# Splitting the projection weights in pieces of 512 columns, and taking the top-k passes ahead of two conv slabs

## What is computed

```python
(u_pool, c_a, c_g, d_q, d_k, d_v, i_q, i_k, i_w,
 n_q, n_ck, n_cv, n_sk, n_sv, n_wk, n_wv, n_g) = jnp.split(x @ w_in[l], IN_OFFSETS, axis=-1)
y_pool = _pool_mixer(u_pool, ...)            # trailing means over 2/4/8/16 tokens
y_conv = _conv_module(c_a, c_g, ...)         # a*sigmoid(g), causal depthwise conv of width 31, LN, silu, pointwise
y_dsa = _dsa_attention(d_q, d_k, d_v, i_q, i_k, i_w, slopes_dsa)  # top 128 keys by a ReLU indexer
y_nsa = _nsa_attention(...)
mix = jnp.concatenate([y_pool, y_conv, y_dsa, y_nsa], axis=-1)
x = _layernorm(DN_ALPHA * x + mix @ w_out[l], ln1_g[l], ln1_b[l])
gate, up = jnp.split(x @ w_gate_up[l], 2, axis=-1)
x = _layernorm(DN_ALPHA * x + (jax.nn.silu(gate) * up) @ w_down[l], ln2_g[l], ln2_b[l])
```

## Time and profile before

| | |
|---|---|
| times of three runs | 2241.58, 2241.82, 2243.14 us |
| median | 2241.82 us |
| span of the profiled execution | 2238.2 us |
| PE busy | 2139.7 us (96%) |
| DVE busy | 650.7 us (29%) |
| POOL busy | 1258.1 us (56%) |
| ACT busy | 195.1 us (9%) |

### The profile page before, as it was taken

The page is one execution under the profiler, slowest core; times in us unless marked ns, Lnnn a source line. Parts: engine busy times, 40 slices in busy tenths (PEclk is TensorE's granted clock), DMA queues, the critical chain, the costliest instruction groups (busy, mean ns, idle before and its releaser), DMA issues.

```text
span 2238.2 us, 23796 instructions
## 1 busy us (share of the span) xinstructions
PE 2139.7 (96%) x9593; PEld 1742.9 (78%) x9593; DVE 650.7 (29%) x1017; ACT 195.1 (9%) x380; POOL 1258.1 (56%) x447
## 2 busy tenths in 40 slices
PE   8999996399999899999999999999999999999996
PEld 7778885266788788888888888888888888888885
DVE  1037999747100811102011120201111020110217
ACT  2020000046000300000000000000000000000001
POOL 6536665016366366555556656565555656666565
PEclk9999998699999999999999999999999999999998
DMA  6323334021423232333333233332333333232332
GB/s 186 96 74 95 94 94 113 0 81 39 169 94 100 89 94 94 94 96 94 105 98 95 94 94 94 94 94 94 95 103 94 101 94 94 94 94 94 94 94 94
DMA packets 290049, 212.64 MB, mean 95 GB/s; under 512 B 7478, under 2 KB 254070, under 8 KB 288218
## 3 DMA queue, kind: packets, MB, share of 16 engines
q1 hardware_dynamic: 289930, 211.97, 31.8%
q10 hardware_dynamic: 80, 0.13, 0.0%
HBM read 207.76 MB, written 4.19 MB: 95 GB/s over the span
## 4 chain that ended last, share of the span: by engine, by line
PE 84%; DVE 14%; issue 1%; ACT 0%; POOL 0%; DMA 0%; DVEq 0%; POOLq 0%; ACTq 0%
PE psum L580 17%; PE psum L582 16%; PE psum L581 16%; DVE proj L1260 7%; PE psum L917 7%; PE psum L918 7%; PE psum L916 7%; PE psum L811 2%; PE psum L813 2%; PE psum L812 2%; DVE sel L1243 1%; DVE top L1242 1%; PE psum L791 1%; PE psum L729 1%; DVE acc L1472 1%; PE psum L703 1%
## 5 line engine op out<-in xcount | busy, mean ns | idle before, releaser
L457 POOL TENSOR_TENSOR w_lo<-raw,w_hi 128x2048 fp32r<-128x2048 f32 (+1 forms) x175 | 822.0, 4697 | 14.6
L454 POOL TENSOR_SCALAR w_hi<-raw 128x2048 fp32r<-128x2048 f32 (+1 forms) x175 | 338.7, 1935 | 792.7 <-PE psum L582 512.4
L580 PE MATMUL psum<-act_hi,w_hi 128*128 128x512 f32 (+1 forms) x1984 | 764.3, 385 | 5.3 <-DVE act_lo L1192 2.2
L582 PE MATMUL psum<-act_hi,w_lo 128*128 128x512 f32 (+1 forms) x1984 | 762.3, 384 | 0.0
L581 PE MATMUL psum<-act_lo,w_hi 128*128 128x512 f32 (+1 forms) x1984 | 762.2, 384 | 0.0
L580 PEld LDWEIGHTS psum<-act_hi,w_hi 128*128 128x128 f32 x1984 | 372.8, 188 | 82.0 <-DVE act_lo L1480 2.7
L581 PEld LDWEIGHTS psum<-act_lo,w_hi 128*128 128x128 f32 x1984 | 372.7, 188 | 74.9 <-issue 0.5
L582 PEld LDWEIGHTS psum<-act_hi,w_lo 128*128 128x128 f32 x1984 | 372.5, 188 | 74.4
L1517 DVE TENSOR_TENSOR hid<-psum,silu_g 128x512 f32<-128x512 f32 x44 | 30.5, 692 | 840.9 <-PE psum L582 840.9
L918 PE MATMUL psum<-w_lo,h_hi 128*128 128x512 f32 x640 | 253.1, 396 | 0.0
L917 PE MATMUL psum<-w_hi,h_lo 128*128 128x512 f32 x640 | 253.1, 395 | 0.0
(11 more groups left out here) (189 smaller groups left out, 1186.7 us busy)
## 6 DMA issues: line engine op xcount, KB each, us to landing
raw<-in_w_gate_up SPq DMA_DIRECT2D x88, 1024.0 KB, 5.7
raw<-in_w_down SPq DMA_DIRECT2D x44, 1024.0 KB, 5.0
raw<-in_w_in SPq DMA_DIRECT2D x31, 1024.0 KB, 5.6
raw<-in_w_out SPq DMA_DIRECT2D x16, 1024.0 KB, 5.0
proj<-in_x SPq DMA_DIRECT2D x4, 1024.0 KB, 7.8
acc<-in_x SPq DMA_DIRECT2D x1, 4096.0 KB, 12.4
ln_g<-in_ln_g SPq DMA_DIRECT2D x2, 1024.0 KB, 9.3
ln_b<-in_ln_b SPq DMA_DIRECT2D x2, 1024.0 KB, 11.4
```

Of the source, the lines that this page charges most:

```text
L454: nc.gpsimd.tensor_scalar(hi, raw[:, slot, 0:words], 1.0, 1.0, ALU.mult, ALU.mult)\
L457: nc.gpsimd.tensor_tensor(lo, raw[:, slot, 0:words], hi.bitcast(F32), ALU.subtract)\
L580: nc.tensor.matmul(out_ap, stat_hi, mov_hi, start=first, stop=False)
L582: return nc.tensor.matmul(out_ap, stat_lo, mov_hi, start=False, stop=last)
```

## The change

It has two parts. In the loop over slabs 5 to 32 GpSimd splits each slab in four pieces of 512 columns, high then low for each piece, with a wait between the two and none between a piece's low part and the next piece's high part; `hi_done` and `split_done` are counted once, after all four. On VectorE the two last `conv_value` move from ahead of the top-k into it: block 1 goes first, then `conv_value(2)` and block 2, then `conv_value(3)` and block 3.

```diff
+            def split_quarters(slot, loads, n, pieces):
+
+                pool.wait_ge(raw_loaded[slot], loads)
+                pool.wait_ge(slab_done, n - 1)
+                nc.gpsimd.sem_inc(split_begun, 1)
+                for q in range(4):
+                    cols = slice(q * SLAB // 4, (q + 1) * SLAB // 4)
+                    nc.gpsimd.tensor_scalar(w_hi[:, slot, cols], raw[:, slot, cols], 1.0, 1.0, ALU.mult, ALU.mult)\
+                        .then_inc(quarter_hi, 1)
+                    pool.wait_ge(quarter_hi, pieces + (q + 1))
+                    ins = nc.gpsimd.tensor_tensor(w_lo[:, slot, cols], raw[:, slot, cols],
+                                                  w_hi[:, slot, cols].bitcast(F32), ALU.subtract)
+                    ins.then_inc(quarter_lo, 1)
+                pool.wait_ge(quarter_lo, pieces + 4)
+                nc.gpsimd.sem_inc(hi_done, 1)
+                nc.gpsimd.sem_inc(split_done, 1)
+
             with pool.Fori(0, (N_IN - N_CONV) // 2) as c:
-                split(1, c * 16 + 48, 2 * c + N_CONV)
-                split(0, c * 16 + 64, 2 * c + (N_CONV + 1))
+                split_quarters(1, c * 16 + 48, 2 * c + N_CONV, c * 8)
+                split_quarters(0, c * 16 + 64, 2 * c + (N_CONV + 1), c * 8 + 4)
...
-            conv_value(2)
-            conv_value(3)
             ve.wait_ge(relu_used, 3 * IDX_HEADS)
 
             for i in range(1, TT):
+                if i > 1:
+                    conv_value(i)
                 w = (i + 1) * P
```

More of the change, by code:

```diff
@@ L196, in build @@
         split_done = sem("split_done")
+        quarter_hi = sem("quarter_hi")
+        quarter_lo = sem("quarter_lo")
         slab_done = sem("slab_done")
```

## The result

| | before | after |
|---|---|---|
| median | 2241.94 us (four runs) | 2205.28 us (2204.21 to 2206.47, four runs) |
| span of the profiled execution | 2238.2 us | 2202.0 us |
| ratio | | 0.9835, 95% interval 0.9821 to 0.9849 |

A forecast was written before the change was run, and what follows sets the result against it. TensorE bounds nearly everywhere but waits for VectorE's late channel sums; earlier conv and cheaper taps bring its restart from 429.4 to 391, so span 2238.2 - 38.4 = 2199.8, plus 3.6 gives 2203.4 us; range 2190 to 2225.

The forecast's parts named there:

- Where the time is: TensorE idles from 374.2 to 429.4 us, waiting for VectorE's channel sums; VectorE's program up to them is 55 us late.
- Part 1, the order: VectorE's top-k runs without waiting for slabs 10 and 12; conv begins at 206 us, 38 earlier; by itself 18 us gained.
- block ends: A few additions at the ends of VectorE's top-k blocks, put at a loss of half a microsecond.
- Part 2, the pieces: Conv taps wait for shorter GpSimd pieces: 8.7 taps a slab, 1.27 us each, 124 steps in 158 us, ending at 364.
- The mixers: VectorE's mixers and sums after the conv take turns with GpSimd until 386.4 us; channel sums at about 391.
- The sum: TensorE restarts at 391 in place of 429.4: 38 us less, span 2199.8, with 3.6 us around it 2203.4.
- No door: Rival: VectorE can't get in between a low half and the next high half without a wait; 2223 us, chance 0.14.
- TensorE binds: Rival: taps come faster, sums are ready before slab 30 at 375 to 376; gain 53 us, 2189 us, chance 0.09.
- GpSimd binds: Rival: each GpSimd instruction costs 1.3 us more, a split lasts 18 us, a slab 14.8; 2289 us, chance 0.03.
- round-trip formula: Slab time when GpSimd's split sets TensorE's pace: (10.88 + 0.76 + 18) / 2 = 14.8 us for an 18 us split.
- Given back later: Rival: the stages after 429 us do not move, for a wait the trace doesn't show; 2240 us, chance 0.04.
- main case: VectorE and GpSimd take turns at every instruction: 2203.4 us, own range 2199 to 2210, chance 0.70.

The follow-up runs named there:

- part 1 alone: Against the kernel before, only the order on VectorE changed, GpSimd still splitting whole slabs: 2227.25 us, ratio 0.9933.
- two experiments: Against the changed kernel: 15 of 31 conv taps kept (another result), 2185.04 us, restart 376.3; channel sums ahead of the mixers, 2188.97 us, restart 378.3.
- the eighths: The whole change with eight pieces of 256 columns a slab in place of four: 2224.51 us, ratio to the kernel before 0.9918.
- halves: The whole change with two pieces of 1024 columns a slab in place of four: 2220.24 us, ratio to the kernel before 0.9900.
- run with fewer taps: The whole change with 16 of the conv's 31 taps left out (another result): 2185.04 us, ratio to the kernel before 0.9744.

## Why the prediction was right, point by point

**Where the time is.** Right. TensorE waited for VectorE's channel sums only. The restart moved from 429.38 to 393.59, 35.8 us, and the span fell by 36.2. Nothing was given back later.

**Part 1, the order.** The gain in the conv's start was 34.6 us, not 38: the first step stands at 209.68, not 206, and outside the 204 to 208 named as a sign. VectorE never idles between 141 and 206, as said. The term that was off is the block ends, put at half a microsecond. VectorE's timeline of the changed kernel has them:

```profile
156.71 1.47 DVE L1266 TENSOR_TENSOR sel<-sel,dist 128x256 f32<-128x256 f32 x1
158.22 0.69 DVE L1225 TENSOR_TENSOR proj<-psum,proj 128x512 f32<-128x512 f32 x1
158.82 1.36 DVE L1259 TENSOR_TENSOR sel<-sel,cmp_p 128x128 f32<-128x128 f32 x1
...
180.64 1.53 DVE L1266 TENSOR_TENSOR sel<-sel,dist 128x384 f32<-128x384 f32 x1
182.20 0.69 DVE L1225 TENSOR_TENSOR proj<-psum,proj 128x512 f32<-128x512 f32 x1
182.80 1.36 DVE L1259 TENSOR_TENSOR sel<-sel,cmp_p 128x128 f32<-128x128 f32 x1
```

Against 0.43, 0.29, 0.56 and 0.29 us alone these four lose 4.2 us. For part 1 alone I had taken the block ends as free altogether, and there they cost 12: a gain of 14.9 us against 18 to 19. The logits stage gained 0.7 us (I took 1).

**Part 2, the pieces.** The turns are as worked out. The conv's 124 steps took 160.9 us (209.68 to 370.5), 1.30 a step, against 158 and 1.27: two slabs hold 17 steps (232.54 to 254.73), 8.5 a slab and not 8.7. A slab took 11.15 us (GpSimd's starts 232.81 and 255.11 are two slabs apart), against 11.05 (the prediction's 22.0 us for two slabs are 11.02 each; it goes on with 11.05 and 11.07). Slab 30's last matmul was issued at 376.53 and ended at 376.92; 376 was said. The cover of TensorE's delay was there: it cost nothing, as VectorE was later by 17 us.

**The mixers.** Too dear by 4 us: 23 us (370.5 to 393.5) in place of 27. I had every two-input instruction wait its turn as long as GpSimd splits, the shortest too; some of one to three columns slipped through just ahead of a piece (0.16 us at 372.83 and 378.06), while others were held (0.45 us at 372.34). The prediction had named such slipping as a sign of being wrong, with a restart near 384: it is true of a few instructions only, and mixers and sums came out 4 us shorter, not 7.

**The sum.** 3.7 us late at the start, 2.9 in the conv, 4 back in the mixers: restart at 393.6 against 391, 2205.3 against 2203.4. Errors of opposite sign make it look better than its terms, which is luck. The 3.6 us added to the span are also not what lies around it: in the changed kernel's profiled run that is 2.2 us (2204.21 less 2202.0), the rest is scatter between executions.

**The rivals.** "No door" falls by the trace of the changed kernel. The Trainium skill, GPSIMD Engine Reference, section 2.1, on which it leaned, speaks of Pool cores that don't wait for one another; in this case's trace that did not keep VectorE out between two Pool instructions without a wait (taps of 0.97 and 1.65 us in turn). "TensorE binds" did not occur, but its floor of 376 is close to where two experiments found it (restarts at 376.3 and 378.3 without a wait). "GpSimd binds" did not occur; its price was wrong. It used the round-trip formula alone, and the eighths show the other bound: at T = 18 a slab would take 18.5 and not 14.8 us, and the point from which the change loses is a split of about 12.5 us in every slab, not 14.7 (55.4 us over its 26 slabs are 2.1 us a slab, not 2.3, so a slab of 13.0). I had given it 0.03; quarters at 10.7 stand closer to it than I said. "Given back later" did not occur either: restart and span moved by the same 36 us.

**The range** held the time, and so did the narrower 2199 to 2210 of the main case. The two parts were costed from the turns that the trace of before shows; the busy times (GpSimd's 63 us more, VectorE's the same) would not have told that the kernel gets faster.

## What to carry to other kernels

Where two engines block one another by whole instructions, cost an edit by turns: each blocked instruction waits for one of the other's, so the size of the other's pieces is the price, and the engine that splits finer pays a turn for each piece; go finer until that engine's own time for a unit, in turns, reaches the consumer's. Here the best of whole, halves, quarters and eighths was the one that just reached it. Before making a late chain faster, look in it for work that its consumer doesn't need: moving the mixers behind the sums gave as much as either part of the change, with nothing added to the work.

## What the runs showed of the hardware

- In the conv the taps and GpSimd's instructions alternate, also between two GpSimd instructions that no wait separates. The Trainium skill, SBUF — State Buffer, section "SBUF: two separate sides", says that the pair of ports which both share is held exclusively for a whole instruction; this trace agrees, with blocked taps of 4.96, 2.77, 1.66 and 1.10 us beside low halves of 2048, 1024, 512 and 256 columns.
- Which small instructions take part is finer than I knew. VectorE's timeline of the changed kernel, beside GpSimd's pieces at 374.13 (high) and 375.27 (low): the copy of one column isn't held up, that of two columns is. The run with fewer taps shows the same (0.15 us at 289.25, 1.15 at 290.20). The two also read different tiles, so that the width decides is not shown.

```profile
374.82 0.15 DVE L1295 COPY blk<-proj 128x1 f32<-128x1 f32 x1
...
375.76 1.15 DVE L1295 COPY blk<-blk 128x2 f32<-128x2 f32 x1
```

- A turn costs slightly more than hold plus work: at 256 columns high half to high half took 1.90 us beside taps (242.96 to 244.86), 1.86 were worked out, at 512 columns 2.70 against 2.63.
